# Two layers' recurrence levels placed by twos between projection tiles, with a second place for the even levels' factors

## The reference

```python
for l in range(DEPTH):                       # DEPTH = 2
    h = layer_norm(ALPHA * h + 0.5 * swiglu(h, ...))
    z = h @ w_in[l]
    cb, cc, ch, rq, rf, ri, rg, pu = jnp.split(z, split_at, axis=-1)
    y_conv = short_gated_conv(ch, cb, cc, conv_w[l])
    y_rec = hgrn2(rq, rf, ri, rg, lbs[l], rec_norm_g[l])
    y_pool = multiscale_pool(pu, pool_w[l], pool_scale[l])
    mix = jnp.concatenate([y_conv, y_rec, y_pool], axis=-1) @ w_out[l]
    ...                                      # cross attention, second swiglu

# hgrn2: f = lb + (1 - lb) * sigmoid(rf), k = 1 - f, per head
#   o_t = sum over s <= t of  (q_t . k_s . prod_{s < u <= t} f_u)  v_s
```

## Time and profile before

| what | value |
|---|---|
| median of 3 runs | 2385.74 us |
| the three runs | 2388.91, 2385.74, 2385.42 us |
| span of the profiled execution, first to last instruction | 2387.8 us |
| TensorE busy | 2337.8 us (98%) |
| VectorE busy | 1191.2 us (50%) |
| ScalarE busy | 838.1 us (35%) |
| GpSimd busy | 192.9 us (8%) |
| mean granted TensorE clock, share of full | 0.999 |

### The profile page before, as it was taken

How to read it: one execution, slowest core, us unless ns; L and a number is a source line. 1 busy time by engine, 2 the same in 40 slices (tenths; PEclk the granted TensorE clock), 3 DMA queues, 4 the chain that set the end, 5 groups by cost and what they waited for, 6 DMA issues and landing times.

```text
span 2387.8 us, 33233 instructions
## 1 busy us (share of the span) xinstructions
PE 2337.8 (98%) x13482; PEld 1610.3 (67%) x13482; DVE 1191.2 (50%) x1626; ACT 838.1 (35%) x1036; POOL 192.9 (8%) x90
## 2 busy tenths in 40 slices
PE   9999999999999999999999999999999999999998
PEld 8889989888888998988899983333333333333335
DVE  5668866755755886675586873111211111111115
ACT  4454344544444434454448442111111111111113
POOL 0002502200200250220020000000000000000000
PEclk9999999999999999999999999999999999999999
DMA  7665454556566545455646589999999999999995
GB/s 253 219 201 171 159 186 133 193 184 204 177 194 202 169 159 189 133 191 187 201 135 202 168 320 412 428 426 428 428 426 428 428 427 428 427 427 428 428 426 218
DMA packets 221361, 665.31 MB, mean 279 GB/s; under 512 B 10034, under 2 KB 164656, under 8 KB 191553
## 3 DMA queue, kind: packets, MB, share of 16 engines
q1 hardware_dynamic: 221248, 663.71, 73.4%
HBM read 662.63 MB, written 1.05 MB: 278 GB/s over the span
## 4 chain that ended last, share of the span: by engine, by line
PE 81%; DMA 14%; SPq 4%; DVE 1%; issue 0%; ACT 0%; DVEq 0%; ACTq 0%
PE ps L810 19%; PE ps L821 17%; PE ps L787 13%; DMA ring<-in_w_up_dram 12%; PE ps L1468 9%; PE ps L1516 6%; PE ps L908 4%; SPq L481 2%; DMA work<-in_w_down_dram 2%; PE ps L1433 1%; PE ps L1442 1%; SPq L476 1%; PE ps L1022 1%; PE ps L1674 1%; PE ps L1296 1%; SPq L494 1%
## 5 line engine op out<-in xcount | busy, mean ns | idle before, releaser
L2363 DVE TENSOR_TENSOR ring_halves<-ring,ring_halves 128x2048 fp32r<-128x2048 f32 (+1 forms) x214 | 527.1, 2473 | 190.2 <-ACT ring_halves L1774 190.0
L810 PE MATMUL ps<-x_halves,ring_halves 128*128 128x512 f32 (+1 forms) x2560 | 457.1, 339 | 0.0
L1774 ACT CAST ring_halves<-ring 128x2048 fp32r<-128x2048 f32 (+1 forms) x214 | 401.4, 1876 | 117.9 <-PE ps L821 90.5
L810 PEld LDWEIGHTS ps<-x_halves,ring_halves 128*128 128x128 f32 x2560 | 394.4, 188 | 59.3
L2949 DVE TENSOR_TENSOR work<-ps,work 128x256 f32<-128x256 f32 x64 | 26.9, 420 | 632.7 <-PE ps L1502 632.7
L1468 PE MATMUL ps<-ring,work 128*64 128x512 f32 x1248 | 278.1, 595 | 23.6 <-DMA ring<-in_w_up_dram 23.6
L821 PE MATMUL ps<-ring_halves,work_halves 128*128 128x512 f32 x1184 | 288.9, 391 | 0.2
L787 PE MATMUL ps<-x_halves,ring_halves 128*128 128x256 f32 x2208 | 274.8, 285 | 0.1
L787 PEld LDWEIGHTS ps<-x_halves,ring_halves 128*128 128x128 f32 x2208 | 267.7, 192 | 2.1 <-issue 0.7
L821 PEld LDWEIGHTS ps<-ring_halves,work_halves 128*128 128x128 f32 x1184 | 221.4, 188 | 47.3 <-issue 2.3
L1762 ACT COPY hT<-ps 128x512 f32<-128x512 f32 x98 | 57.3, 585 | 506.2 <-PE ps L1468 461.1
(11 more groups left out here) (305 smaller groups left out, 2336.3 us busy)
## 6 DMA issues: line engine op xcount, KB each, us to landing
ring<-in_w_up_dram SPq DMA_DIRECT2D x77, 2048.0 KB, 40.1
work<-in_w_up_dram SPq DMA_DIRECT2D x37, 2048.0 KB, 40.3
ring<-in_w_down_dram SPq DMA_DIRECT2D x36, 2048.0 KB, 40.3
ring<-in_w_in_dram SPq DMA_DIRECT2D x52, 1024.0 KB, 5.3
ring<-in_ffn_up_dram SPq DMA_DIRECT2D x44, 1024.0 KB, 5.3
ring<-in_ffn_down_dram SPq DMA_DIRECT2D x44, 1024.0 KB, 5.0
ring<-in_ffn_gate_dram SPq DMA_DIRECT2D x43, 1024.0 KB, 5.4
work<-in_w_down_dram SPq DMA_DIRECT2D x19, 2048.0 KB, 39.7
```

The lines of the kernel that those rows point to most:

```text
L810: mm = pe.matmul(out, wt[:, o:o + P], x, start=(k == 0 and n == 0), stop=(k == DT - 1 and n == 1))
L1774: nc.scalar.copy(second_half(high_of(name)[:], name), second_half(ring[:, s, :], name))\
L2363: v.tensor_tensor(second_half(ring_halves[s][:], name), second_half(ring[:, s, :], name), second_half(high_of(name)[:].bitcast(F32), name) ...
```

## The change

TensorE's order in the mixer is, before: `cc`, level 0, `ch`, level 1, `cb`, level 2, `pu`, level 3, `ri0`, `ri1`, level 4, `ck0`, level 5, `ck1`, level 6, `ck2`, level 7, `ck3`, level 8. After: `cc`, `ch`, levels 0 and 1, `cb`, `pu`, levels 2 and 3, `ri0`, `ri1`, levels 4 and 5, `ck0`, `ck1`, levels 6 and 7, `ck2`, `ck3`, level 8. For two levels in a row two sets of factors must stand at once, so even levels write theirs to `VM`, a stretch of 2048 columns that at this point holds nothing, and `factors(lv)` waits for level lv-2. VectorE's order is rewritten to match. `VM` is set to zero once at the start.

```diff
+        def factor_at(tag, lv):
+            return (VM, VM + 1024) if tag[0] == "r" and lv % 2 == 0 else (FQ, FK)
...
-                    kk, qq = fk, fq
+                    qq, kk = (w(o, 1024) for o in factor_at(tag, lv))
...
                 pe.wait_ge(dve_done.sem, dve_done.at(("k", L)))
+                by_columns(("ch", L), 1)
                 level(r, 0)
-                by_columns(("ch", L), 1)
                 level(r, 1)
                 by_columns(("cb", L), 0)
+                by_columns(("pu", L), 1)
                 level(r, 2)
-                by_columns(("pu", L), 1)
                 level(r, 3)
...
                 level(r, 4)
+                level(r, 5)
                 for j in range(4):
                     by_columns((f"ck{j}", L), j % 2, mh, ml)
-                    level(r, 5 + j)
+                    if j == 1:
+                        level(r, 6)
+                        level(r, 7)
+                level(r, 8)
...
-                if lv >= 2:
-                    pe_group(("A", tag, lv - 1, 1))
+                reader = lv - 2 if tag[0] == "r" else lv - 1
+                if reader >= 1:
+                    pe_group(("A", tag, reader, 1))
...
                 advance(r, 1)
-                scores_out(r, 0)
...
-                for lv, names in ((2, ("ch",)), (3, ("cb",)), (4, ("pu",)), (5, ("ri0", "ri1")), (6, ("ck0",)),
-                                  (7, ("ck1",)), (8, ("ck2",))):
+                for lv, first, names in ((2, (0, 1), ("ch",)), (4, (2, 3), ("cb", "pu")), (6, (4, 5), ("ri0", "ri1")),
+                                         (8, (), ("ck0", "ck1"))):
                     factors(r, lv)
+                    if lv < 8:
+                        advance(r, lv)
+                        factors(r, lv + 1)
+                    else:
+                        mine(("F", r, lv))
+                    if first:
+                        scores_out(r, first[0])
                     for nm in names:
                         next_low((nm, L))
                     if lv < 8:
-                        advance(r, lv)
-                    else:
-                        mine(("F", r, lv))
-                    scores_out(r, lv - 1)
+                        advance(r, lv + 1)
+                        scores_out(r, first[1])
+                next_low(("ck2", L))
+                scores_out(r, 6)
+                for t in range(TT):
+                    bank_empty(6 + t, ("A", r, 6, t))
+                scores_out(r, 7)
                 last_scores(r)
...
-                        v.memset(w(UP, 516), 0.0), v.memset(w(PU, 544), 0.0)):
+                        v.memset(w(UP, 516), 0.0), v.memset(w(VM, 2048), 0.0), v.memset(w(PU, 544), 0.0)):
```

More of the change, by code:

```diff
@@ L2534, in factors @@
                 (_, q1), (k0, _), (_, p1), (s0, _) = (splits(o, n) for o in (Q, K, PR, SU))
-                fq1, fk0 = splits(FQ, n)[1], splits(FK, n)[0]
-                if lv >= 2:
-                    pe_group(("A", tag, lv - 1, 1))
+                at = factor_at(tag, lv)
+                fq1, fk0 = splits(at[0], n)[1], splits(at[1], n)[0]
+                reader = lv - 2 if tag[0] == "r" else lv - 1
+                if reader >= 1:
+                    pe_group(("A", tag, reader, 1))
                 v.tensor_tensor(fq1, q1, p1, ALU.mult)
```

## The result

The changed kernel takes 2394.57 us (median of 6 runs, 2393.14 to 2395.8) where the kernel before takes 2386.89 (median of 6 runs, the three shown and three more, 2385.42 to 2388.91). The ratio is 1.0031 with a 95% interval of 1.0021 to 1.0041: slower, by 7.7 us. The forecast was 2390.8, slower by 5.1 us, in a range up to 2395.0, so the measured time lies 0.4 us inside the end of the range. The direction and the place of the loss were right, and a third of the loss was not in the sum.

A forecast was written before the change was run, and what follows sets the result against it. TensorE, busy 98%, was taken as the bound. Per layer, waits 1.95 us + GpSimd 1.8 + bank 0.15 - 1.36 saved gave +2.5, two layers +5.1, on the median 2385.74: 2390.8 us, range 2386.0 to 2395.0.

The forecast's parts named there:

- What the pairing removes: In each mixer layer, levels stand in four places instead of eight, at 0.34 us each: 1.36 us saved.
- The low half of `ri1`: At `ri1`, TensorE waits 1.1 us for a low half queued on VectorE behind factors of level 4.
- The low half of `ck1`: At `ck1`, TensorE waits 0.85 us for a low half behind the same row of VectorE work.
- What GpSimd takes: GpSimd's operations slow VectorE's in the two chains ahead of the low halves: 0.9 us a chain.
- Level 5's bank: Scores of level 3 come about when level 5 wants its banks: priced at 0.15 us a layer.
- The sum: Span 2387.8 - 2.7 + 7.8 = 2392.9 us; put on the median, 2385.74 + 5.1 = 2390.8 us.
- the lock: Rival: every operation of VectorE's chains fully meets one of GpSimd's; at most +9.2 us more, 2400, likelier 2395; chance 0.13.
- The floor (1): Rival: stalls at both low halves stay at their least, GpSimd out of the way; +1.2 us, 2386.9; chance 0.27 with milder forms.
- VectorE keeps up (2): Rival: VectorE brings the low halves in time and the gain stays whole; -2.7 us, 2383.0; chance 0.05.
- the second level pays (4): Rival: a pair's second level pays 0.2 to 0.3 us for its semaphores, leaving 0.7 of 2.7 us; 2392.9; chance 0.09.
- Edits at nothing: Early `ch`, banks of levels 2 and 3, `ck2`'s low half before level 8, memset, transfers: priced at no cost.

The follow-up runs named there:

- early_lows: The changed kernel with the low halves of `ri1` and `ck1` moved ahead of factors(4) and factors(6) on VectorE; 2384.48 us, ratio 0.9989; again 2383.88 us, 0.9986.
- low_before_scores: The changed kernel with one low half of each group (`ri0`, `ri1`, `ck1`) put ahead of the pair of scores before it; 2390.56 us, ratio 1.0014.
- place_only: The kernel before with the second place for even levels' factors, the new factors' wait and the memset, levels in old positions; 2387.76 us, ratio 1.0001.
- quiet_gpsimd2: The changed kernel with GpSimd's short convolution and pooling each replaced by a memset, so its result is not valid; 2390.3 us, ratio 1.001.

## Why the prediction was right, and where it was short

- **What the pairing removes, 1.36 us a layer.** Right: the pair is 2.02 us, two tiles behind it 11.71, and `early_lows` has the gain by itself, 1.34 us in the chain.
- **The low half of `ri1`, at least 1.1 us.** Right in mechanism, and near in size: 1.0 without GpSimd, 1.26 with it.
- **The low half of `ck1`, at least 0.85 us.** Right: 0.8 without GpSimd, 1.91 with it.
- **What GpSimd takes, 0.9 us a chain.** That GpSimd takes time from VectorE was right. The 1.8 us a layer is a third too much against the measured 1.35, and it is spread wrongly: 0.25 and 1.1. The two operations of 1.23 and 1.22 us in the earlier trace rows were not met again at level 4, where GpSimd, which had run on during VectorE's wait, was mostly at a scaling; their like came in the second chain, where level 7's factors took 1.00 and 1.23 us beside two tensor operations of GpSimd:

```profile
269.83 1.00 DVE L2549 TENSOR_TENSOR work<-work 128x512 f32<-128x512 f32 x1
270.75 1.23 DVE L2550 TENSOR_TENSOR work<-work 128x512 f32<-128x512 f32 x1
```

```profile
269.32 0.95 POOL L3250 TENSOR_TENSOR work<-work 128x265 f32<-128x265 f32 x1
270.36 1.07 POOL L3251 TENSOR_TENSOR work<-work 128x257 f32<-128x257 f32 x1
```

- **Level 5's bank, 0.15 us.** Not seen in the changed kernel: no wait of TensorE at a level stands in its list of waits. Where TensorE came 0.7 us earlier, in `low_before_scores`, it was 0.45 us.
- **The sum.** The step that was short is the one that put a layer at 1.95 + 1.8 + 0.15 - 1.36. It counted a stop of TensorE as its own length, and so put its price beyond that at nothing. Measured: waits of 1.26 + 1.91, then 0.3 and 0.2 us for the tiles to get going again (5.74 where `ri1` takes 5.4, 5.99 where a tile takes 5.76), then 1.48 us in which `ck1` ran partly at half clock, less 1.36: 3.8 us. The clock was in no term. The profile of before could have named it: its one stop of 1.5 us, in the experts, is followed by a fall that cost 1.7 us. The mixer itself had no stop from which to price one.
- **What was luck.** The waits came to 1.26 and 1.91 us, 6.3 in all, where 1.5 to 2.5 each and 7 to 8 in all had been named. What the sum had too much, 0.45 us for GpSimd and 0.15 for the bank in each layer, hid part of the 2 us a layer that it lacked. And the upper part of the range, in which the result lies, was there for the lock and was filled by the clock and the slow starts.
- **The rivals.** The floor (1) fell because GpSimd's operations are there; without them its waits are seen, but not its time. That VectorE keeps up (2) fell by the waits; its gain came in `early_lows`. The lock (3), every meeting a full one, fell although nearly every operation of the chains met one of GpSimd's: beside a scaling, like the one below behind S, VectorE's took 0.68 to 0.85 us, and only beside tensor operations in the second chain 1.00 and 1.23. That the second level pays (4) fell by the 2.02 us.

```profile
252.36 1.89 POOL L3228 TENSOR_SCALAR work<-work,taps 128x256 f32<-128x256 f32 x1
```

- **Edits at nothing.** Early `ch`, the banks, the memset, level 8: no wait is seen at any of them, and in `place_only` the memset brought no new wait.

## What to carry to other kernels

When a saturated engine's work is regrouped, the gain is the count of changes between kinds of work times their price, here 0.34 us, and it is small; the risk is in the queue of the engine that feeds it. Put what the busy engine needs next ahead of an instruction that waits for that engine, into the feeder's idle time: two low halves moved turned +7.7 us into -2.5. Price a stop of TensorE at more than its length: here 0.2 to 0.4 us in the tile behind it, and 1.5 us more in four of the six stops of 1.9 to 2.2 us, behind which the clock fell. Look for such falls in the profile of before, also outside the part that changes.

## What the runs showed of the hardware

- In the mixers TensorE's granted clock fell to 0.50 behind an idle time of 1.9 us (three times out of four in two profiles) and of 2.2 us (once out of two), and never behind 0.6 to 1.4 us (16 stops), nor where 1.78 us of fp32 matmuls stood in place of the wait. It cost 1.5 us of `ck1` each time. In the experts it fell once in the eleven profiles behind the stop of 1.5 us that all of them have. And in `quiet_gpsimd2` and `low_before_scores` it fell at 2357 us, where TensorE had not stood idle for more than 0.2 us at once just before. So a stop is not the only thing that brings a fall, and what decides is left open.
- A tile that starts after a stop takes 0.2 to 0.4 us longer at full clock: 5.99 us for 48 matmuls in place of 5.76, and 5.73 to 5.78 for the 24 of `ri1` in place of 5.4.
- A level of 16 small fp32 matmuls costs 0.93 us between others of its kind, and 0.34 us more where it stands between fp32r tiles.
- An operation of GpSimd can last far longer than any one of VectorE's beside it. A scaling that takes 0.92 to 1.25 us elsewhere took 5.17 us beside two low halves and the advance behind them (GpSimd's timeline of the changed kernel), while the two low halves took their usual 4.48 us and the first operation of the advance 0.88, 0.2 more than usual. Beside a single low half of VectorE, in `low_before_scores`, such a scaling took 2.85 us. That it is held off by them is inferred from these times, and those of GpSimd are rough:

```profile
273.17 5.17 POOL L3243 TENSOR_SCALAR work<-work,cnt 64x256 f32<-64x256 f32 x1
```
